# A feed-forward up projection from seven block products on quarters of weights and activations

## The reference, cut to what matters

```
h2  = rmsnorm(x, g_ffn) * (1 + scale2) + shift2          # 1024 tokens x 1024 channels
up  = h2 @ w_up                                          # w_up: 1024 x 5632
up  = up[t-1]*w[0] + up[t]*w[1] + up[t+1]*w[2] + bias    # per channel, along the tokens
act, lin = split(up, 2)                                  # 2816 channels each
y   = x + gate2 * ((gelu(act) * lin) @ w_down)           # w_down: 2816 x 1024
```

## Time and profile before

| | us |
|---|---|
| median of three runs (2950.53 to 2953.08) | 2952.98 |
| the profiled execution, its own time | 2951.98 |
| its span, first to last instruction | 2950.2 |
| PE busy | 2868.6 (97%) |
| DVE busy | 1409.3 (48%) |
| ACT busy | 691.5 (23%) |
| POOL busy | 634.6 (22%) |
| mean granted TensorE clock, share of full | 0.986 |

### The profile page before, as it was taken

The page is one execution under the profiler, slowest core; times in us unless marked ns, Lnnn a source line. Parts: engine busy times, 40 slices in busy tenths (PEclk is TensorE's granted clock), DMA queues, the critical chain, the costliest instruction groups (busy, mean ns, idle before and its releaser), DMA issues.

```text
span 2950.2 us, 34297 instructions
## 1 busy us (share of the span) xinstructions
PE 2868.6 (97%) x13183; PEld 2332.4 (79%) x13183; DVE 1409.3 (48%) x1748; ACT 691.5 (23%) x702; POOL 634.6 (22%) x288
## 2 busy tenths in 40 slices
PE   5999999999899999999989999999989999999998
PEld 2788888888688888888878888888868888888886
DVE  4363736445644433444476445353754443444435
ACT  4111111111522222222261111111142222222222
POOL 0211221222222211212222221212222222222212
PEclk7999999999999999999999999999999999999999
DMA  9301111110111111111131110201101111111112
GB/s 381 99 24 52 43 45 42 43 44 28 65 57 57 43 50 43 44 48 43 43 129 45 43 44 28 59 21 52 42 29 57 50 43 43 46 55 55 43 50 79
DMA packets 205572, 170.03 MB, mean 58 GB/s; under 512 B 7761, under 2 KB 182625, under 8 KB 202465
## 3 DMA queue, kind: packets, MB, share of 16 engines
q1 hardware_dynamic: 200641, 151.74, 16.6%
q10 hardware_dynamic: 4896, 17.83, 1.6%
HBM read 161.15 MB, written 8.39 MB: 57 GB/s over the span
## 4 chain that ended last, share of the span: by engine, by line
PE 91%; DVE 4%; DMA 2%; ACT 1%; issue 1%; POOL 0%; DVEq 0%; SPq 0%; POOLq 0%; ACTq 0%
PE ps L469 64%; PE ps L663 12%; PE ps L477 6%; PE ps L518 2%; DVE a_hi L1550 1%; DMA ada<-in_w_ada 1%; PE ps L692 1%; PE ps L708 1%; PE ps L679 1%; PE ps L709 1%; DVE cl L1541 1%; DVE cl L1538 1%; PE ps L721 1%; ACT cl L992 1%; PE ps L500 1%; PE ps L499 1%
## 5 line engine op out<-in xcount | busy, mean ns | idle before, releaser
L1038 POOL TENSOR_TENSOR w_lo<-w_raw,w_hi 128x1024 fp32r<-128x1024 f32 x238 | 577.9, 2430 | 2143.5 <-ACT w_hi L798 2143.5
L469 PE MATMUL ps<-h_hi,w_hi 128*128 128x512 f32 x2216 | 685.5, 391 | 4.6 <-DVE h_lo L1149 4.6
L469 PE MATMUL ps<-h_lo,w_hi 128*128 128x512 f32 x2216 | 682.5, 389 | 0.0
L469 PE MATMUL ps<-h_hi,w_lo 128*128 128x512 f32 x2216 | 682.4, 389 | 0.0
L469 PEld LDWEIGHTS ps<-h_hi,w_hi 128*128 128x128 f32 x2216 | 413.5, 188 | 90.2 <-ACT h_hi L853 5.4
L469 PEld LDWEIGHTS ps<-h_lo,w_hi 128*128 128x128 f32 x2216 | 416.0, 188 | 86.7
L469 PEld LDWEIGHTS ps<-h_hi,w_lo 128*128 128x128 f32 x2216 | 416.0, 188 | 86.6
L1158 DVE SCALAR_TENSOR_TENSOR xT<-ps,modT,xT 128x1024 f32<-128x1024 f32 x240 | 302.7, 1282 | 186.9 <-PE ps L469 127.2
L798 ACT ACTIVATE w_hi<-w_raw 128x1024 fp32r<-128x1024 f32 x238 | 250.2, 1055 | 432.3 <-PE ps L663 148.3
L1538 DVE SCALAR_TENSOR_TENSOR ca<-ps,convS,ca 128x1023 f32<-128x1023 f32 x44 | 56.5, 1283 | 439.8 <-ACT ca L992 439.8
L663 PE MATMUL ps<-w_hi,h_hi 128*128 128x512 f32 x512 | 200.6, 392 | 6.9 <-DVE h_lo L1149 5.6
(11 more groups left out here) (166 smaller groups left out, 3170.8 us busy)
## 6 DMA issues: line engine op xcount, KB each, us to landing
w_raw<-in_w_in SPq DMA_DIRECT2D x56, 512.0 KB, 3.8
ada<-in_w_ada SPq DMA_DIRECT2D x24, 1024.0 KB, 8.6
w_raw<-in_w_up SPq DMA_DIRECT2D x44, 512.0 KB, 3.8
w_raw<-in_w_down SPq DMA_DIRECT2D x44, 512.0 KB, 3.7
w_raw<-in_w_up SPq DMA_DIRECT2D x88, 192.0 KB, 2.8
w_raw<-in_w_in SPq DMA_DIRECT2D x68, 128.0 KB, 2.3
w_raw<-in_w_in SPq DMA_DIRECT2D x34, 256.0 KB, 3.0
xin<-in_x ACTq DMA_DIRECT2D x16, 512.0 KB, 6.5
```

Of the source, the lines that this page charges most:

```text
L469: ins = pe.matmul(ps[:, slot, b * HALF:(b + 1) * HALF], w[:, w_slot, col:col + P], a[:, k, b * HALF:(b + 1) * HALF], start=first and n == ...
L1038: pool.tensor_tensor(w_lo[:, ws, :], w_raw[:, i % 2, :], w_hi[:, ws, :].bitcast(F32), ALU.subtract).then_inc(lo_done.sem, 1)
```

## The change

The up projection of one hidden block (its activated and its linear half, called a *set*, 22 in a sequence) is a product of a 2 x 2 block matrix of weights with a 2 x 2 block matrix of activations. The weight quarters are (activated or linear half) x (input channels 0 to 511 or 512 to 1023); the activation quarters are (channels 0 to 511 or 512 to 1023) x (tokens 0 to 511 or 512 to 1023). Eight quarter products were made. Now it is seven, each of 4 channel blocks x 3 passes = 12 matmuls, on quarters and sums of quarters, and the four quarters of the result are put together from the seven by additions.

- Activations: `hc_hi` and `hc_lo` hold seven pieces (three plain quarters, four sums), each of 4 blocks x 512 tokens, made once per sequence in `mid` (`scale_mid`, `b_low`, `t_sums`, `t_low` on DVE; `modulate_mid` and copies on ACT).
- Weights: blocks arrive in `f_raw` (4 slots). Each of the seven pieces of a set is rounded by ACT (`piece_high`) and its remainder taken by POOL (`piece_low`) into `f_w`, a ring of five pieces of 512; POOL also makes the four sums of quarters, in place in `f_raw`. The down projection takes four such pieces for a pair of sets.
- Results: PE puts the seven products of a set into four banks (`PRODUCT_BANK`), three of them used twice. ACT copies two products out (`copy_t`, `copy_u22`), DVE makes seven additions of 512 (`sum_u11` to `sum_u21`) into `u_sb`. The convolution's taps now read `u_sb` in SBUF, not PSUM.
- The rounded product for the down projection is now made by ACT from the full one (`a_high`); DVE makes the full one (`gated`) and the remainder (`a_low`).
- The order of sets and down projections is `FFN_ITEMS`: set 2g, down g-1, set 2g+1. A down projection thus runs one pair of sets later than its inputs. PE's `down` uses two PSUM slots in turn and waits, from its third step, for the residual update of two steps before. On DVE the linear half's side taps and product stand between the first residual updates.
- The first two sets are interleaved by hand with the norm (`opening_sets`).
- `Fori` loops are unrolled in all engines, and all large tiles stand at fixed offsets, whole KiB from a base that is a multiple of 512 (`at`).

The core of the difference:

```diff
-                with pe.Fori(0, GROUPS) as g:
-                    where = ("ffn", seq, g)
-                    two_units(where, mid)
-                    for i in (2, 3):
-                        pe.wait_ge(*res_done.at(where, i - 3))
-                        unit(where, i, f"U{i}")
-
-                    partial(where, 4, a_hi, a_lo, ahi_done, alo_done,
-                            [side_tap.at(where, 2 * i + 2) for i in range(4)])
+                where = ("ffn", seq, 0)
+                opening_sets(where, mid)
+                for kind, n in FFN_ITEMS:
+                    if kind == "set":
+                        ordinary_set(where, n)
+                    else:
+                        down(where, n)
...
+            def product_row(seq, s, i, w, k):
+                piece = PRODUCT_PIECE[i]
+                high, low = hc_hi[seq][:, piece, k, :], hc_lo[seq][:, piece, k, :]
+                cols = slice(k * P, (k + 1) * P)
+                for n, (a, b) in enumerate(((w[0], high), (w[1], high), (w[0], low))):
+                    ins = pe.matmul(bank_of(s, i), a[:, cols], b, start=k == 0 and n == 0,
+                                    stop=k == KQ - 1 and n == 2)
...
+            def ordinary_set(where, s):
+                last = s - 1 if s > 2 else 0
+                pe.wait_ge(*summed["t"].at(where, last + 1))
+                product(where, s, 0)
+                pe.wait_ge(*summed["u21a"].at(where, last + 1))
+                product(where, s, 1)
+                pe.wait_ge(*summed["u12a"].at(where, last + 1))
+                product(where, s, 2)
+                pe.wait_ge(*summed["u21"].at(where, last + 1))
+                product(where, s, 3)
+                pe.wait_ge(*t_copied.at(where, s + 1))
+                product(where, s, 4)
+                pe.wait_ge(*summed["u11"].at(where, s + 1))
+                product(where, s, 5)
+                pe.wait_ge(*u22_copied.at(where, s + 1))
+                product(where, s, 6)
...
+            def down(where, g):
...
+                        if r >= 2:
+                            pe.wait_ge(*res_done.at(where, r - 1))
...
+            def piece_high(where, q):
...
+                if q >= WEIGHT_RING:
+                    act.wait_ge(*piece_used(where, q - WEIGHT_RING))
...
+            def piece_low(where, q):
...
+                a11, a12, a21, a22 = (piece_raw(PIECE_NO[kind, n, m]) for m in (0, 1, 3, 6))
+                if i == 0:
+                    pool.wait_ge(*loaded(where, (kind, n, 1)))
+                    pool.tensor_tensor(a21, a21, a22, ALU.add).then_inc(s1_set.sem, 1)
...
+                    pool.tensor_tensor(a11, a21, a11, ALU.subtract).then_inc(s2_set.sem, 1)
+                elif i == 1:
...
+                    pool.tensor_tensor(a12, a12, a11, ALU.subtract).then_inc(s4_set.sem, 1)
+                elif i == 4:
...
+                    pool.tensor_tensor(a11, a22, a11, ALU.subtract).then_inc(s3_set.sem, 1)
...
+            def ordinary_sums(where, s):
+                sum_u11(where, s)
+                sum_u12(where, s)
+                side_before(where, s, 0)
+                side_after(where, s, 0)
+                sum_u22(where, s)
+                sum_u21(where, s)
...
+                        for d in range(KC):
+                            if before[0] == "set":
+                                if d == 0:
+                                    side_before(where, s, 1)
+                                elif d == 1:
+                                    side_after(where, s, 1)
+                                elif d == 2:
+                                    gated(where, s)
+                            down_residual(where, n, d)
```

More of the change, by code:

```diff
@@ L80 @@
              ("last", 1))
-    TIMES = {"first": 1, "mix": PAIRS, "mid": 1, "ffn": GROUPS, "swap": 1, "last": 1}
+    TIMES = {"first": 1, "mix": PAIRS, "mid": 1, "ffn": 1, "swap": 1, "last": 1}
     def __init__(self, sem, setup=0, **per):
@@ new lines, in product @@
+            def product(where, s, i):
+                w = weight_piece(where, ("set", s, i))
+                for k in range(KQ):
+                    product_row(where[1], s, i, w, k)
+            def ordinary_set(where, s):
[14 more added lines that the diff above has]
+                product(where, s, 6)
@@ L519, in turn, with spread_mid @@
                 ins.then_inc(full[slot].sem, 1)
+            def spread_mid(where):
+                for b in range(2):
+                    pe.wait_ge(*diag_done.at(where, b + 1))
+                    pe.matmul(ps_row[:, (3 + b) * HALF:(4 + b) * HALF], ones[:, :], diag_mid[:, b * HALF:(b + 1) * HALF],
+                              start=True, stop=True).then_inc(spread.sem, 1)
             def partial(where, block0, act_hi, act_lo, hi_t, lo_t, slot_read):
@@ L921, in _ @@
                     store_y(swap, 7)
-                with act.Fori(0, PAIRS) as pr:
+                    act.wait_ge(*down_done.at(swap, 0))
+                    split(("mix", 1, 0), 1)
+                for pr in range(PAIRS):
                     where = ("mix", seq, pr)
```

764 lines of the change are left out of this document (552 added, 212 removed), and 2 rows, old and new, of the table STEPS.

## The result

| | before | after |
|---|---|---|
| median of the runs made together, us | 2951.80 (4 runs) | 2993.45 (4 runs, 2992.42 to 2996.34) |
| span of the profiled execution, us | 2950.2 | 2992.0 |
| mean granted clock in that span | 0.986 | 0.959 |

The ratio is 1.0143 (95% interval 1.0125 to 1.016): the change makes the kernel 1.4% slower. I had forecast 2920 us, in a range of 2860 to 2985, and given slower 0.27.

A forecast was written before the change was run, and what follows sets the result against it. PE was taken as the bound, busy 2868.6 of 2950.2 us. The span 2950.2 - 119.7 - 10.4 - 16.7 + 20 + 12 + 82 = 2917.4 us gave a forecast time of 2920 us, range 2860 to 2985.

The forecast's parts named there:

- Matmuls removed: Up projection: 84 matmuls a set instead of 96, 528 fewer at 0.2267 us each, -119.7 us; unrolling costs nothing.
- The rival that dense products might fail: Up projection: products of 12 matmuls with three waits and a new bank run less densely; 2953 us, chance 0.06.
- Wait for the gated tile: Feed-forward passes: PE's 0.47 us wait for `a_hi` goes in all 22 passes, -10.4 us.
- Distance of matmuls: Down projection and mixer's output projection: one grid of 512 brings matmuls from 0.2325 to 0.2267 us, -16.7 us.
- Steady sets: Pairs of sets with a down projection: late DVE work makes PE wait 4.1 us a pair, +82 us, bounds 14 and 158.
- The residual update 3.4 late at the third step: Each steady down projection: DVE's chain, lengthened by POOL, makes PE's third step wait 3.4 us for this update.
- the 0.7 for `u11`: Even set of each steady pair: the chain ahead of `u11` makes the sixth product 0.7 us late.
- the port costs more: Steady pairs: POOL gets in before each of five DVE operations, 7 us a pair; 2978 us, chance 0.16.
- POOL's effect on DVE: Steady sets: DVE operations with both inputs in SBUF wait for POOL, lengthening four by 0.2, 0.65, 1.2 and 0.7 us.
- Openings: Activations in `mid`: work starts 7.8 us later, plus 2.2 for a later clock rise, twice: +20 us; bounds 3 and 16 a sequence.
- First ordinary set: Set 2: ten queued DVE operations of 1.2 to 1.3 us delay its first sum, 5 to 6 us a sequence, +12 us.
- The rest: Swap and last norm: costed at nothing, the second mixer's first two weight blocks being split between squares ACT must do anyway.

The follow-up runs named there:

- e12: The kernel of e3 with GpSimd's feed-forward operations cut to 16 columns as in e6: 2834.42 us.
- e4: The kernel before, with a 128-byte pad so that mixer and feed-forward activation tiles share the weights' offset within 512 bytes: 2941.34 us, 0.9969 of before.
- e8: The kernel of e3 with every tile from `w_split` upward moved up by 128 bytes per partition: 2939.72 us, 33.8 more than e3.
- e7: The changed kernel with 15 unused matmuls ahead of the third-step wait in each down projection but the last two: 2972.34 us.
- e10: The changed kernel with only GpSimd's sums of weight quarters cut to 16 columns from the sixth weight piece on: 2913.24 us.
- e6: The changed kernel with GpSimd's feed-forward remainders and sums cut to 16 columns from the sixth weight piece on: 2858.51 us.
- e2: The changed kernel with ScalarE splitting the second mixer's second weight block ahead of the norm's scaling: 2983.83 us.
- e1: The changed kernel with VectorE making each residual update ahead of a convolution piece in the down projections: 2915.17 us, 0.9874 of before.
- e3: The changed kernel with the edits of e1 and e2 together: 2905.89 us, 0.9842 of before.
- e5: The kernel of e3 with set 2's first sum and its copy of `u22` moved forward in each sequence: 2902.12 us.
- e9: The kernel of e5 with set 2's side taps put between the first residual updates of the first down projection: 2889.70 us, 0.9786 of before.

## Why the prediction was wrong

- *Matmuls removed, -119.7.* Right: 12655 matmuls, and e12 shows them at 0.2267 in the new form, unrolled. The rival that dense products might fail is excluded.
- *Wait for the gated tile, -10.4.* Right: no such wait is left.
- *Distance of matmuls, -16.7.* Right, with the cause shown by e4 and e8. The rule of the Trainium skill that I had set against it (TensorE: Matmul & The Clock Gate, "Step-by-step: what each phase is for"), two independent read ports, would make both experiments come out at no change; they measured -10 and +34 us, and the measurement decides.
- *Steady sets, 4.1 us a pair: here the forecast failed*, by 2.1 us a pair (66.04 less 59.85 is 6.2). The residual update 3.4 late at the third step was right in place, cause and size (57.2 us in 20 waits). Of the 0.7 for `u11` about 0.4 came (in the first pair that product starts 0.24 us late, and its next step 0.1), and other small waits made up the rest and a little more. What was left out is the clock. I had priced a later rise of the clock in the openings, where PE stands for 6 us in the trace of before, and never asked what a stop of 3.4 us does in each pair that I had just put there: another 2.0 us (e7; e10's stops give 1.6 for one of 1.8 us), 28 us in the fourteen pairs of the windows. With it the step would have been 6.1, the sum 2960, and the case that I called *the port costs more*, deciding from 5.8 us a pair, would have come true by another mechanism.
- *POOL's effect on DVE.* The mechanism was right: e6 takes the side taps back to 1.28 us and the 2048-column operations to 2.29 without a change on DVE. The four lengthened operations of the pair shown add up to 2.7 us, as my timetable had it, so the size of the wait was no luck. The Trainium skill says (SBUF — State Buffer, "Who interferes with whom") that a VectorE instruction with two SBUF inputs contends with a GpSimd instruction that reads SBUF. The rows agree: `u12`, with two such inputs, lasts 1.27 us instead of 0.69, and the residual update, with one, 1.28 as before. The effect was weighed in the steady sets only.
- *Openings, 10 us a sequence, were 16.* The term that failed is the four sums and four remainders at 2.2 us each: beside POOL's weight pieces seven of the eight last 3.3 to 3.4 us. e6 gives 7.6 us back. It is the bound of 16 that I had kept, by another cause than I gave for it.
- *First ordinary set, 5 to 6 us, was 14.7.* The ten operations that I counted at 1.2 to 1.3 us last up to 2.2 beside POOL (e6: 7.7 us back), and the stop of 12.4 us puts the clock at 0.80 in this stretch.
- *The rest, at nothing.* Wrong by 12.4 us: I named the squares that hide the splits of the swap, but the second split stands behind the norm's eighteen scaling operations, and PE needs it after 48 matmuls. The order of ACT's queue says so; it needed no trace of the changed kernel. e2 takes 9.6 us of it back.
- Not forecast at all: 10.1 us at set 21, which follows set 20 with no down projection between (two waits of 5.1 us for `u_sb` in the two sequences together, there in e1, e3, e5, e7 and e9 alike). In e10 it is 0.4 us a sequence, and in e6 and e12 it is gone, so it comes with POOL's weight pieces and sums. Whether through DVE's longer operations or through the pieces' own lateness was not separated.

Summed up, of the 78.8 us: 29 are the fourteen pairs (2.09 each, 2.0 of it the clock), 30 the openings and first sets, 12 the swap, 14 the last stretches (10 of it at set 21), and the first pair of each sequence, which has no wait, gives 6 back.

## What to carry to other kernels

A wait that a change adds to a dense stretch of matmuls is to be priced with what the granted clock does behind it; here 3.4 us of standing cost 5.4. When work is moved from PSUM to SBUF on DVE, or given to POOL, list what stands beside it: cutting POOL's work in the feed-forward part to a few columns was worth 10 us before and 135 us after. And read each queue in order: the updates that release the busiest engine belong ahead of work that has time, and four reorderings of two queues (e1, e2, e5, e9) made a loss of 1.4% a gain of 2.1%.

## What the runs showed of the hardware that I had not expected

- The offset of the stationary against the moving tile within 512 bytes sets the distance of matmuls: 0.2267 us with both at 0, 0.2272 with both at 128 (e8's down projection), 0.2325 with 384 bytes between them before, 0.2333 with 128 in e8.
- 270 useless matmuls made the kernel 21 us faster (e7).
- Of eight stops of 1.8 us in e10, three were followed by a fall of the clock and five were not.
- A second side tap right behind the first lasts 1.95 us on the mean with or without POOL's sums, and 1.28 only when its remainders go too.
